# RWKV-7 group norm tail: weight and bonus term put on in token layout by GpSimd, one turn to channels instead of two, at another place in the written order

## The reference, cut to what matters

```python
y = rwkv7_recurrence(rh, heads(decay), kh, vh, -kk, kk * heads(a))
mean = jnp.mean(y, axis=-1, keepdims=True)
var = jnp.mean(jnp.square(y - mean), axis=-1, keepdims=True)
y = ((y - mean) * lax.rsqrt(var + GN_EPS)).reshape(Bsz, T, C) * ln_w + ln_b
bonus = jnp.sum(rh * kh * r_k, axis=-1, keepdims=True) * vh
y = y.astype(h.dtype) + bonus.reshape(Bsz, T, C)
return (y * g) @ w_o, v_first
```

## Time and profile before

| | |
|---|---|
| three runs | 2577.1, 2584.65, 2585.39 us |
| span of the profiled execution | 2577.7 us |
| PE busy | 2504.1 us, 97% |
| DVE, ACT, POOL busy | 859.3, 953.4, 991.0 us |
| recurrence, about 565 to 845 us | of its last 250 us PE is busy 216.59 us |

### The profile page before, as it was taken

How to read it: one execution, slowest core, us unless ns; L and a number is a source line. 1 busy time by engine, 2 the same in 40 slices (tenths; PEclk the granted TensorE clock), 3 DMA queues, 4 the chain that set the end, 5 groups by cost and what they waited for, 6 DMA issues and landing times.

```text
span 2577.7 us, 46700 instructions
## 1 busy us (share of the span) xinstructions
PE 2504.1 (97%) x18778; PEld 2053.7 (80%) x18794; DVE 859.3 (33%) x1300; ACT 953.4 (37%) x1572; POOL 991.0 (38%) x470
## 2 busy tenths in 40 slices
PE   8999999999888999999999999999999998999998
PEld 6888877777776788888888888888888777788887
DVE  5222036455554332210433122221054567322200
ACT  4233225534543343321443333332153565333321
POOL 4444453322222354444443444444454101444442
PEclk9999999988988999999999999999999999999999
DMA  4333222210000233322243443333232241333321
GB/s 153 95 97 98 98 82 98 74 34 4 4 4 25 77 107 97 98 98 98 94 152 123 142 144 98 98 98 98 95 110 90 66 127 55 98 98 98 98 96 59
DMA packets 181773, 230.37 MB, mean 89 GB/s; under 512 B 16408, under 2 KB 119992, under 8 KB 181624
## 3 DMA queue, kind: packets, MB, share of 16 engines
q1 hardware_dynamic: 181624, 228.20, 27.9%
HBM read 213.47 MB, written 14.68 MB: 89 GB/s over the span
## 4 chain that ended last, share of the span: by engine, by line
PE 83%; issue 11%; POOL 2%; DVE 2%; ACT 2%; DMA 0%; SPq 0%; POOLq 0%; ACTq 0%; DVEq 0%
PE bank L343 19%; PE bank L345 19%; PE bank L344 19%; PE bank L350 5%; PE bank L352 5%; PE bank L351 5%; POOL w_lo L318 2%; PE bank L1353 1%; PE bank L1240 1%; PE bank L1323 1%; PE bank L1371 1%; PE bank L990 1%; PE bank L1823 1%; DVE xg_lo L1803 1%; PE bank L1555 1%
## 5 line engine op out<-in xcount | busy, mean ns | idle before, releaser
L318 POOL TENSOR_TENSOR w_lo<-w_raw,w_hi 128x1024 fp32r<-128x1024 f32 x376 | 906.8, 2416 | 1309.3 <-ACT w_hi L313 1308.5
L313 ACT ACTIVATE w_hi<-w_raw 128x1024 fp32r<-128x1024 f32 x376 | 395.4, 1058 | 1008.9 <-PE bank L345 860.4
L343 PE MATMUL bank<-xg_hi,w_hi 128*128 128x512 f32 x1408 | 550.1, 391 | 5.7 <-POOL w_lo L318 3.1
L345 PE MATMUL bank<-xg_hi,w_lo 128*128 128x512 f32 x1408 | 548.6, 390 | 0.0
L344 PE MATMUL bank<-xg_lo,w_hi 128*128 128x512 f32 x1408 | 548.5, 390 | 0.0
L343 PEld LDWEIGHTS bank<-xg_hi,w_hi 128*128 128x128 f32 x1408 | 264.8, 188 | 63.6 <-issue 7.6
L344 PEld LDWEIGHTS bank<-xg_lo,w_hi 128*128 128x128 f32 x1408 | 264.7, 188 | 55.7 <-issue 0.7
L345 PEld LDWEIGHTS bank<-xg_hi,w_lo 128*128 128x128 f32 x1408 | 264.7, 188 | 54.6
L343 PE MATMUL bank<-hid_hi,w_hi 128*128 (+1 forms) x704 | 274.4, 390 | 0.0
L345 PE MATMUL bank<-hid_hi,w_lo 128*128 (+1 forms) x704 | 273.9, 389 | 0.0
L344 PE MATMUL bank<-hid_lo,w_hi 128*128 (+1 forms) x704 | 273.9, 389 | 0.0
(11 more groups left out here) (290 smaller groups left out, 3142.5 us busy)
## 6 DMA issues: line engine op xcount, KB each, us to landing
w_raw<-in_ffn_w_in SPq DMA_DIRECT2D x352, 256.0 KB, 3.0
w_raw<-in_ffn_w_out SPq DMA_DIRECT2D x176, 256.0 KB, 2.7
w_raw<-in_w_kv SPq DMA_DIRECT2D x96, 256.0 KB, 3.1
w_raw<-in_rwkv_w_rkv SPq DMA_DIRECT2D x48, 256.0 KB, 2.9
w_raw<-in_attn_w_q SPq DMA_DIRECT2D x48, 256.0 KB, 3.1
k_dram<-stage SPq DMA_DIRECT2D x6, 1024.0 KB, 4.6
v_dram<-stage SPq DMA_DIRECT2D x6, 1024.0 KB, 5.5
keys<-k_dram SPq DMA_DIRECT2D x24, 256.0 KB, 3.4
```

What stands on the lines that cost most here:

```text
L313: act.activation(w_hi[:, s, :], w_raw[:, s, :], ACT.Copy).then_inc(w_hi_ready, 1)
L318: pool.tensor_tensor(w_lo[:, s, :], w_raw[:, s, :], w_hi[:, s, :].bitcast(F32), ALU.subtract).then_inc(w_lo_ready, 1)
L343: pe.matmul(o, hi, x_hi, start=start, stop=False)
L345: return pe.matmul(o, lo, x_hi, start=False, stop=stop)
```

## The change

`ytp` turns one tile in place of two. In token layout `ln_w` is not one number per partition but a row of 64, so it is loaded by two small DMAs, broadcast over the partitions, into a tile `ln_w`. Two new steps behind `ynorm` work on `yt` in place: `weigh` multiplies by `ln_w`, and `joined` adds `bv`. Both are POOL's; for the last pair alone they are DVE's (`weigh_last`, `joined_last`). `bvp` and `ysb` are gone. `ys` adds only `ln_b`. `ytp`, `gp` and `ys` stand together behind `z` of the last chunk. The three POOL steps count one semaphore, `tail`. The load of `ln_w` waits until the last product of the value projection.

```diff
-    inv+1.2 root-1.0 state+0.4 zs+0.5 rk+2.0 lift+1.3 arr+2.0 decay+0.5 z+0.5 pend+2.0 u+0.5 gs+1.3 ynorm-1.0
-    uscan+2.0 us+0.5 join+1.3 s+0.5 ytp-1.0 state+0.5 uscan+2.1 z+0.6 xs+1.3 bsp+2.0 flip+1.3 ys-1.0 bvp-1.0 inv+1.3
-    zs+0.6 lift+1.4 us+0.6 u+0.6 bs+2.0 s+0.6 bkb+2.0 gs+1.4 decay+0.6 ysb-1.0 state+0.6 join+1.4 bkk+2.0 z+0.7
-    gp-1.0 xs+1.4 zs+0.7 u+0.7 flip+1.4 bv+0.0 us+0.7 yg-1.0 ylo-1.0 s+0.7 ub+2.0 inv+1.4 zs+1.0 lift+1.5
+    inv+1.2 root-1.0 state+0.4 zs+0.5 rk+2.0 lift+1.3 arr+2.0 decay+0.5 z+0.5 pend+2.0 u+0.5 gs+1.3 ynorm-1.0 weigh-1.0 joined-1.0
+    uscan+2.0 us+0.5 join+1.3 s+0.5 state+0.5 uscan+2.1 z+0.6 xs+1.3 bsp+2.0 flip+1.3 inv+1.3
+    zs+0.6 lift+1.4 us+0.6 u+0.6 bs+2.0 s+0.6 bkb+2.0 gs+1.4 decay+0.6 state+0.6 join+1.4 bkk+2.0 z+0.7
+    ytp-1.0 gp-1.0 ys-1.0 xs+1.4 zs+0.7 u+0.7 flip+1.4 bv+0.0 us+0.7 yg-1.0 ylo-1.0 s+0.7 ub+2.0 inv+1.4 zs+1.0 lift+1.5
...
+            sp.wait_ge(w_used, c0 + 3 * KT)
+            for hh in range(2):
+                src = a["rwkv_ln_w"][0].rearrange("(q h d) -> h q d", h=2, d=HD)[hh].unsqueeze(0)
+                sp.dma_start(ln_w[head(1 - hh)], src.to_broadcast([CH, KT, HD])).then_inc(lora_landed, 16)
...
         def bv_pool(pool, q, _):
             after_read(pool, q, "bs")
-            work_full(pool, q - 1, "bv")
+            need(pool, "tail", q - 1)
             done(pool.tensor_tensor(bv[:, :, :], v2[:, q], bs[:, q % 4, :].unsqueeze(2).to_broadcast([P, NC, CH]),
-                                    ALU.mult), "bv")
+                                    ALU.mult), "tail")
+
+        def weigh_pool(pool, q, _):
+            if q == 0:
+                pool.wait_ge(lora_landed, 16 * 8)
+            need(pool, "gn", q)
+            done(pool.tensor_tensor(chunks(yt[:, :]), chunks(yt[:, :]), ln_w[:, q].unsqueeze(1).to_broadcast([P, NC, CH]),
+                                    ALU.mult), "tail")
...
+        def joined_pool(pool, q, _):
+            need(pool, "tail", q, 2)
+            done(pool.tensor_tensor(yt[:, :], yt[:, :], flat(bv[:, :, :]), ALU.add), "tail")
...
         def ytp_pe(pe, q, _):
-            need(pe, "gn", q)
+            need(pe, "tail", q)
             turn_rows(pe, q, "yt", lambda rows, c: yt[rows, c * CH:(c + 1) * CH])
-
-        def bvp_pe(pe, q, _):
-            need(pe, "bv", q)
-            turn_rows(pe, q, "bv", lambda rows, c: bv[rows, c, :])
...
-            read_work(act.activation(ys[:, :], work_bank(q, "yt")[:, :], ACT.Identity, bias=col("rwkv_ln_b", q),
-                                     scale=col("rwkv_ln_w", q)), q, "yt")
-
-        def ysb_dve(dve, q, _):
-            after_read(dve, q, "yt")
-            work_full(dve, q, "bv")
-            read_work(dve.tensor_tensor(ys[:, :], ys[:, :], work_bank(q, "bv")[:, :], ALU.add), q, "bv")
```

More of the change, by code:

```diff
@@ L68, in rwkv_steps @@
     steps[last + 1:last + 1] = [("wop", pairs - 1, k) for k in range(2)]
-    steps[steps.index(("ylo", pairs - 1, 0))] = ("ylast", pairs - 1, 0)
+    for kind, behind in (("weigh", "ynorm"), ("joined", "weigh_last"), ("ylo", "yg")):
+        steps.remove((kind, pairs - 1, 0))
+        steps.insert(steps.index((behind, pairs - 1, 0)) + 1, (f"{kind}_last", pairs - 1, 0))
     return steps
@@ L131, in build @@
             with ExitStack() as c2:
-                (tw, ta, dec, undec, resets, pcum, yt, ysq, ys, state, decayed, zs, us, cst, bs, btok, ktok, inv_u, inv_g, bv,
+                (tw, ta, dec, undec, resets, pcum, yt, ysq, ys, state, decayed, zs, us, cst, bs, btok, ktok, inv_u, inv_g, ln_w, bv,
                  _, ar, sel, ucum, kk, tk, pend) = tensors(
@@ L226, in build @@
             zv=NC, yv=NC, kv=NC - 1, z=NC - 1, zs=NC, u=NC, us=NC, read_out=NC - 1, st=NC - 1, decayed=NC - 2,
-            state=NC - 1, y=NC, yt=1, gn=6, ysq=1, root=1, bv=1, y_hi=1, y_lo=1)
+            state=NC - 1, y=NC, yt=1, gn=6, tail=3, ysq=1, root=1, y_hi=1, y_lo=1)
         S = {name: sem(f"rwkv_{name}") for name in EVENTS}
@@ L1042, in build @@
         WORK = dict(zwza=["zw", "za"], kkp=["kk"], bsp=["bs"], ub=["ub"], uk=["uk"], btp=["btok"], ktp=["ktok"],
-                    ytp=["yt"], bvp=["bv"], gp=["gate"])
+                    ytp=["yt"], gp=["gate"])
         work_order = [(0, "zw"), (0, "za"), (0, "kk")]
@@ L1544, in bv_pool, with weigh_dve, joined_dve @@
             after_read(pool, q, "bs")
-            work_full(pool, q - 1, "bv")
+            need(pool, "tail", q - 1)
             done(pool.tensor_tensor(bv[:, :, :], v2[:, q], bs[:, q % 4, :].unsqueeze(2).to_broadcast([P, NC, CH]),
-                                    ALU.mult), "bv")
+                                    ALU.mult), "tail")
[5 more added lines that the diff above has]
+                                    ALU.mult), "tail")
+        def weigh_dve(dve, q, _):
+            dve.wait_ge(lora_landed, 16 * 8)
+            need(dve, "tail", q, 1)
+            need(dve, "gn", q)
+            done(dve.tensor_tensor(chunks(yt[:, :]), chunks(yt[:, :]), ln_w[:, q].unsqueeze(1).to_broadcast([P, NC, CH]),
+                                   ALU.mult), "tail")
+        def joined_dve(dve, q, _):
+            need(dve, "tail", q, 2)
+            done(dve.tensor_tensor(yt[:, :], yt[:, :], flat(bv[:, :, :]), ALU.add), "tail")
+        def joined_pool(pool, q, _):
+            need(pool, "tail", q, 2)
+            done(pool.tensor_tensor(yt[:, :], yt[:, :], flat(bv[:, :, :]), ALU.add), "tail")
         def turn_rows(pe, q, w, tile):
@@ L1559, in ytp_pe, with gp_pe @@
         def ytp_pe(pe, q, _):
-            need(pe, "gn", q)
+            need(pe, "tail", q)
             turn_rows(pe, q, "yt", lambda rows, c: yt[rows, c * CH:(c + 1) * CH])
-        def bvp_pe(pe, q, _):
-            need(pe, "bv", q)
-            turn_rows(pe, q, "bv", lambda rows, c: bv[rows, c, :])
+        def gp_pe(pe, q, _):
+            work_free(pe, q, "gate")
+            pe.matmul(work_bank(q, "gate")[:, :], lora2[HD:P, 1, q * P:(q + 1) * P], lora_u[HD:P, 1],
+                      start=True, stop=True).then_inc(work_done, 1)
         def ys_act(act, q, _):
@@ L1569, in ys_act @@
             need(act, "y_lo", q - 1)
[L1570 to L1576 removed]
+            read_work(act.activation(ys[:, :], work_bank(q, "yt")[:, :], ACT.Identity, bias=col("rwkv_ln_b", q)), q, "yt")
         def gp_pe(pe, q, _):
@@ L1600, in build @@
         STEP_PE = dict(zwza=zwza_pe, kkp=kkp_pe, bsp=bsp_pe, ub=ub_pe, uk=uk_pe, btp=btp_pe, ktp=ktp_pe,
-                       lift=lift_pe, flip=flip_pe, join=join_pe, open=open_pe, z=z_pe, u=u_pe, s=s_pe, ytp=ytp_pe,
-                       bvp=bvp_pe, gp=gp_pe)
+                       lift=lift_pe, flip=flip_pe, join=join_pe, open=open_pe, z=z_pe, u=u_pe, s=s_pe, ytp=ytp_pe, gp=gp_pe)
         STEP_ACT = dict(tw=tw_act, ta=ta_act, dec=dec_act, undec=undec_act, pend=pend_act, tk=tk_act, decay=decay_act, bs=bs_act,
@@ L1607, in build @@
                         arr=arr_dve, amb=amb_dve, amk=amk_dve, gs=gs_dve, xs=xs_dve, state=state_dve,
-                        ysum=ysum_dve, ycen=ycen_dve, yvar=yvar_dve, ynorm=ynorm_dve, ysb=ysb_dve, yg=yg_dve, ylast=ylast_dve)
-        STEP_POOL = dict(kp=kp_pool, bkb=bkb_pool, bkk=bkk_pool, rk=rk_pool, odd=odd_pool, bv=bv_pool, ylo=ylo_pool)
+                        ysum=ysum_dve, ycen=ycen_dve, yvar=yvar_dve, ynorm=ynorm_dve, weigh_last=weigh_dve, joined_last=joined_dve, yg=yg_dve, ylo_last=ylast_dve)
+        STEP_POOL = dict(kp=kp_pool, bkb=bkb_pool, bkk=bkk_pool, rk=rk_pool, odd=odd_pool, bv=bv_pool, weigh=weigh_pool, joined=joined_pool, ylo=ylo_pool)
         def pool_masks(pool):
@@ L1717, in rwkv_pe @@
             need(pe, "yt", PAIRS_H - 1)
-            for w in ("yt", "bv", "gate"):
+            for w in ("yt", "gate"):
                 after_read(pe, PAIRS_H - 1, w)
```

8 lines of the change are left out of this document (4 added, 4 removed).

## The result

| | before | after |
|---|---|---|
| median of 12 runs side by side | 2580.44 us | 2586.32 us |
| lowest and highest | 2576.04, 2585.39 | 2580.61, 2590.19 |
| ratio after to before | | 1.0024, 95% interval 1.0013 to 1.0034 |
| the same once more, in a later set of runs | 2579.62 us | 2586.83 us, ratio 1.0023 (1.0011 to 1.0036) |

The changed kernel is slower by 6 us, 0.24%. The forecast was +4.6 us, and 2589.3 us for the time; measured are +6.2 us by the ratio and 2586.32 us, inside the range and inside the 0.3%. The profiled execution's span is 2583.4 us, against 2577.7, and its own time 2585.14 us.

What follows compares the result with a forecast made beforehand. PE's fixed order of steps, with waits between, was taken to set the recurrence's time. The terms -1.1 + 6.0 - 0.3 = +4.6 us, added to 2584.65 us, gave 2589.3 us, range 2580 to 2597 us.

Steps and rivals of the forecast that it cites:

- The frame: In the recurrence, PE does its steps in a fixed order and waits between them; no size of its own.
- PE's work is the limit: Rival: each turn taken out is worth what it occupies, the moved turn costs nothing; -8.4 us, 2576.3 us; chance 0.10.
- The bv turn: Between `flip` and `lift`: removal worth nothing in six rounds, hidden in the wait for `inv`; -1.1 us behind the last pair.
- The turn in the second place: `yt` turn behind `z` of chunk 7: `u` at z+2.4 instead of z+1.41, +1.0 us a round, +6.0 us in six.
- this clock as a rival: Rival: PE's clock stays low longer, some 12 us more at the lower level; +10 us, 2595 us; chance 0.14.
- The working had `state` start when `s` let it: Taking `ysb` off DVE, ahead of `state`, was worth nothing: `state` started when `s` let it, within 0.1 us.
- The first place: `yt` turn gone ahead of `z`, `flip` earlier, but `uscan` waits for `weigh`: -0.3 us; -3.2 us without that wait.
- the scans don't wait for POOL: Rival: `uscan` is not held by `weigh`, so the first place gives -3.2 us; +1.7 us, 2586.4 us; chance 0.24.
- The last chunks: Last pair: two turns leave the chain, one returns ahead of the last `u`; taken as nothing, bounds 0.88 us either way.

Runs made afterwards that it cites:

- the filler: Changed kernel plus 16 matmuls of a turn's size between `flip` and `lift` of level 4, middle pairs only; ratio 1.0024 to the kernel before.
- the kernel with both edits: Changed kernel with both `uscan` halves moved behind `xs` of level 3 and the `yt` turn between `flip` and `lift`; ratios 0.9972 and 0.9983 to the kernel before.

## Why the prediction came out

**The frame held.** PE does its steps in a fixed order, and a step is worth what its place makes it: the same 16 matmuls cost nothing in the slot before `lift` (removed, or added as a filler) and about 1 us in the second place at full clock. With PE at 97% busy, that had to be read from a round. The rival "PE's work is the limit" is out by two experiments, the bv turn removed and the filler.

**The bv turn, 0 in six rounds and -1.1 us behind the last pair.** The 0 was right: 0.53 us from `inv` to `lift` with and without it, and +0.3 us (-3.4 to +3.6) when it alone is removed. The -1.1 us is too small to be seen in any of the runs.

**The turn in the second place, +6.0 us: the mis-sized term.** It measured +10.2 us over the six rounds, 11.0 in one pair of profiles and 9.5 in the other. The count at full clock was right: 2.37 us where 2.3 to 2.4 were forecast, and 0.95 us times six is 5.7 us. What was missing is that the turn runs there at the lower clock in five of six rounds, up to 1.92 us instead of 1.10. The prediction had this clock as a rival with a chance of its own, but as more time at the lower level in the whole stretch, worth +10 us. By its own signs it came: a mean clock of 0.85 or less was to decide for this rival, and it is 0.83 and 0.85; a move by more than 0.03 was to make the forecast wrong, and it fell by 0.05 in the first pair and 0.01 in the second (0.88 and 0.86 before). The +10 us did not come. The two profiles of the kernel with both edits, 0.81 and 0.86, show that such a sign is too weak to decide by.

**From `lift` to `z`, which the forecast put at nothing: -2.5 us.** More than half of the miss came back here, by something that the forecast hadn't in it: PE's idle time without a visible wait, 2.9 and 4.1 us, is gone. Part is also `ysb`. The working had `state` start when `s` let it, to within 0.1 us; at full clock it starts 0.50 to 0.52 us behind `s` of chunk 6 with `ysb` ahead of it on DVE, and 0.38 without, 0.13 us in most of the rounds. The lower clock worked against both. That the total came out near the forecast is to this extent luck.

**The first place, -0.3 us.** Measured -0.5 us on the means, -1.2 in one pair of profiles and +0.3 in the other, and -0.3 more from `flip` to `lift`. Both parts stood up apart: -0.35 us a round without the collision (1.71 against 2.06 us), and +0.44 with it in four rounds (2.50 against 2.06), where the working had +0.57, +0.44, 0.0 and +0.55 for the rounds at full clock. The round for which it was worked out, the first, is not among them: `flip` is 2.02 us behind `s` there, 0.04 sooner than before instead of 0.57 later, and the second half of `uscan` takes 1.07 us, not 1.52. In the two rounds at the lower clock it expected nearly 1 us back each; that hung on spells that another execution puts elsewhere.

**The scans wait.** The rival "the scans don't wait for POOL" fell: 1.52 us beside `weigh`, 1.30 beside another product, 0.69 alone. The forecast for the second half was 1.2 to 1.7 us and for `weigh` 1.6 to 1.7 (1.59 measured; 1.53 in one round). The price depends on cover: 3.2 us by the rounds in the changed kernel (7 by the runs, with 4 us of doubt), 0.2 in the kernel before. The Trainium skill, SBUF — State Buffer, Who interferes with whom, has the whole instruction waiting for the shared port. These rows agree: the second half of `uscan` ends 0.56 us behind `weigh`, and where two halves meet `joined`, the second ends 0.55 us behind that.

**The last chunks, 0 within 0.88 us.** In the changed kernel the last `u` comes 4.33 us behind its `z` (829.08, 833.41) and 3.58 in the other profile, against 1.43 before, so the second place costs up to 2.9 us here too, over three times the bound set for it. From the `u` at the end of the six rounds to the last one it is 26.40 and 25.65 us, against 25.26 and 26.48 before: nothing net, inside the bound, because the rest of these chunks gave as much back.

**The range and the chances.** 2586.32 us lies 3 us under the forecast. The starting point was 4.2 us too high, since the median of the three runs shown was 2584.65 and that of the twelve beside the changed kernel 2580.44; the change itself, 5.9 us by the medians, was 1.3 us larger than forecast. So the two errors partly cancel in the time, and of the change the second place alone would have missed by 4.2 us.

## What to carry to other kernels

Where an engine's order is written by hand, price a step by its place: look for the wait that it can hide in, and check that nothing waits for its results there. Work put into the chain costs there nearly its full length (0.95 us of 1.10), and at a lowered clock nearly twice that, wherever it stood before. Before a product is put on POOL, see what DVE does beside it: a scan there is held for the whole product, and whether that costs anything depends on what is queued behind the scan; moving two scans behind the one step that was waited for took back about all that the change had cost. And look for idle time without a wait in the rows too: here it moved by as many microseconds as the change did.

## What the runs showed of the hardware

- **A scan on DVE and a product on POOL alternate by whole instructions**: a scan half takes 0.69 us alone, 1.52 us beside `weigh`, and two halves with `joined` between them take 2.53 us in all. `xs`, which has one operand in PSUM, kept 0.39 to 0.42 us throughout, also beside `joined`.
- **The clock at one place repeats, its sum doesn't.** One kernel had PE at the lower level for 112.5 and for 78.6 us between 560 and 870 us, with own times of 2586.34 and 2573.75 us. Yet the turn in the second place ran at it, wholly or in part, in five of six rounds of both profiles of the changed kernel, in four and five rounds of the other two kernels that have it there without a filler, and in none with the filler. Where the level fell inside a window shown (668 to 670 us), PE was busy without a gap. Why it falls there is open.
- **PE idles for short times without a wait that the profile shows**: 8.8 and 9.7 us of 184 in the kernel before, 2.9 in both profiles of the changed one. From `lift` to `z` of chunk 7 it had 2.9 and 4.1 us of it before and none after, with the same steps of PE in that stretch. In the kernel without the bonus it fell from 7.0 to 2.0 us when the turn of `yt` (and `ys` on ACT) was moved. What makes it is open.
